# First attention of a two-block transformer kernel: turning the probabilities with a scaled identity, and alternating score and value passes

## The chip, the core and the metric

One core of one Trainium2 chip runs the whole program. The metric is the device time of one execution in microseconds (us). Of the kernel before, three timed runs gave 1631.95, 1635.49 and 1636.21 us; their median is 1635.49 us.

## The reference, cut to what matters

Two transformer blocks run one after the other on 512 tokens of width 1024. The change touches only the attention of the first block: 8 heads of 64 channels, chunks of 64 queries that see their own chunk and the 8 chunks before it, a relative bias, a softmax, and the product with the values.

```python
def one_chunk(c):
    ...
    s = jnp.einsum('bqhd,bkhd->bhqk', qb, kb).astype(jnp.float32) * scale + bias
    valid = (c * CHUNK + kpos - pad) >= 0
    s = jnp.where(valid[None, None], s, NEG_INF)
    p = jax.nn.softmax(s, axis=-1)
    return jnp.einsum('bhqk,bkhd->bqhd', p.astype(vb.dtype), vb)
```

The result goes, beside a pooled half of the channels (`multiscale_pool`), into the output projection `w_out`. Everything is float32.

## The kernel before, in words

**Split matmuls.** A float32 product that must keep its precision is made of three passes (`split3`, lines 347, 350 and 351): both operands are held as a high part and a low part in the type F32R, and the passes are high by high, high by low and low by high, all added up in one PSUM bank. One pass is one weight load (LDWEIGHTS, row PEld of the profile) and one MATMUL. Matmuls on plain F32 operands (`pe.matmul` with `CI(...)`) and transposes (`pe.transpose`) are used where the data isn't split.

**The attention loop.** A unit `u` is one query tile of 128 tokens of one head: `h, q = divmod(u, 4)`, 32 units in all. Its scores are 128 queries by `n = (q + 1) * 128` keys. The loop runs over `u` from 0 to 39 on every engine; each engine has its own list, in order, and semaphores join them. For one `u` TensorE (PE) does:

- `a_scores(u)`: three passes whose contraction has 64 rows (the head's channels; rows 0 to 63 for even heads, 64 to 127 for odd ones), into bank 4 or 5, with `n` columns;
- `side_steps`: one `split3` of 512 columns and 128 rows for the projection `u` (the pooled half), in 24 of the units: not where `u % 10` is 8 or 9, and not from `u = 30` on;
- `a_bias`, once in four units: the next head's bias through a flip matrix, bank 2;
- `a_spread_sums(p)`, at `u` = 11, 19, 27 and 35: the inverse sums of a pair of heads are spread to all partitions by 8 matmuls, bank 2;
- `weigh_values(h, k)` for `u - 7`: three passes with 128 rows and `(4 - k) * 128` columns, into bank 0 or 1;
- `turn_probs` for `u - 2`: `q + 1` transposes of 128x128 of the probabilities `a_p`, bank 6 or 7.

VectorE (DVE) does for one `u`: `a_min_of(u)` (bias added to the scores, minimum of the row; line 1261), then, once in eight units, `a_invert` (reciprocal of 8 columns of sums), `turned_lo(u - 3)` (low part of the turned probabilities, line 1282), and at some units `a_norm` (head output by the inverse sums, line 1276), `a_pair_lo` (line 1288), a part of the pooling, and the weights' low halves (line 1086).

ScalarE (ACT) does `a_expo(u)` (the exponential, line 751, with the sums as a by-product), `turned_hi(u - 2)` (line 759), and at some units `a_spread_copy` (line 770, the spread inverses out of bank 2), `a_pair_hi` (line 774), bias copies and the weights' high halves (line 595).

Behind the loop four `split3` of `poolw` and the eight column tiles of `out1` follow. The second block's attention uses `turn_probs` and `weigh_values` too.

Of the kernel before, what the change touches and what calls it, by code (L numbers as in the profile page):

```python
# [19 lines left out]
ALU = mybir.AluOpType  # L20
# [105 lines left out]
def build(nc, t):  # L126
    with ExitStack() as ctx:
# [68 lines left out]
        with ExitStack() as s:  # L196
# [8 lines left out]
            with ExitStack() as s2:  # L205
                a_s = sb("a_s", [P, 2, S], F32, s2)
                a_p = sb("a_p", [P, 3, S], F32, s2)
                bias = sb("bias", [P, 2, S], F32, s2)
                a_min = sb("a_min", [P, 4 * HEADS], F32, s2)
                a_sum = sb("a_sum", [P, 4 * HEADS], F32, s2)  # L210
                a_rec = sb("a_rec", [P, 4 * HEADS], F32, s2)
                a_full, a_bc = sq, sq_sum
# [246 lines left out]
        a_recip, a_spread, a_spread_out, a_normed = sem("sums_inverted"), sem("inverses_spread"), sem("inverses_copied"), sem("head_out_normed")  # L459
# [88 lines left out]
        def _(act):  # L548
# [217 lines left out]
            def a_spread_copy(p):  # L766
                act.wait_ge(a_spread, p + 1)
                if p >= 2:
                    act.wait_ge(a_normed, 2 * p - 2)
                act.copy(a_bc[:, p % 2, :], bank[2][:]).then_inc(a_spread_out, 1)  # L770

            def a_pair_hi(p):
                act.wait_ge(a_normed, 2 * p + 2)
                act.copy(part[1][:, p, :], a_full[:, p % 2, :]).then_inc(a_ohi, 1)

            for u in range(4 * HEADS + 8):
# [16 lines left out]
            a_pair_hi(3)  # L793
# [274 lines left out]
        def _(dve):  # L1068
# [196 lines left out]
            def a_invert(p):  # L1265

                dve.wait_ge(a_exp, 8 * p + 8)
                dve.reciprocal(a_rec[:, 8 * p:8 * p + 8], a_sum[:, 8 * p:8 * p + 8]).then_inc(a_recip, 1)

            def a_norm(h):  # L1270
                r = 64 * (h % 2)
                dve.wait_ge(a_out, h + 1)
                dve.wait_ge(a_spread_out, h // 2 + 1)
                if h >= 4:
                    dve.wait_ge(a_olo, h // 2 - 1)
                dve.tensor_tensor(a_full[r:r + 64, h // 2 % 2, :], bank[h % 2][r:r + 64, :], a_bc[r:r + 64, h // 2 % 2, :],
                                  ALU.mult).then_inc(a_normed, 1)
# [7 lines left out]

            def a_pair_lo(p):
                dve.wait_ge(a_ohi, p + 1)
                dve.tensor_tensor(part[1][:, 8 + p, :], a_full[:, p % 2, :], part[1][:, p, :].bitcast(F32), ALU.subtract).then_inc(a_olo, 1)
# [14 lines left out]
            for u in range(4 * HEADS + 8):  # L1303
                if u < 4 * HEADS:
                    a_min_of(u)
                if u >= 9 and u % 8 == 1:
                    a_invert(u // 8 - 1)
                if 3 <= u < 4 * HEADS + 3:
                    turned_lo(u - 3, a_thi, a_tlo)
                if u >= 12 and u % 4 == 0 and u % 8 == 4:  # L1310
                    a_norm(2 * (u // 8 - 1))
                if u >= 15 and u % 8 == 7:
                    a_norm(2 * (u // 8 - 1) + 1)
                if u >= 17 and u % 8 == 1:
                    a_pair_lo(u // 8 - 2)
# [6 lines left out]
            a_pair_lo(3)  # L1322
# [463 lines left out]
        def _(pe):  # L1786
# [208 lines left out]
            def a_bias(h):  # L1995
# [4 lines left out]
                if h >= 4 and h % 2 == 0:  # L2000
                    pe.wait_ge(a_spread_out, h // 2 - 1)
# [3 lines left out]
            def a_scores(u):  # L2005
                h, q = divmod(u, TT)
                n, r = (q + 1) * P, 64 * (h % 2)
                if u >= 2:
                    pe.wait_ge(a_biased, u - 1)
                if u == 1:  # L2010
                    pe.wait_ge(acc_free, RES["u"] + 1)
                rows_ = slice(r, r + 64)
                qt, kt = h // 2, 4 + h // 2
                split3(pe, bank[4 + u % 2][:, 0:n], part[1][rows_, qt, q * P:(q + 1) * P], part[1][rows_, 8 + qt, q * P:(q + 1) * P],
                       part[1][rows_, kt, 0:n], part[1][rows_, 8 + kt, 0:n], True, True).then_inc(a_score, 1)

            def a_spread_sums(p):

                pe.wait_ge(a_recip, p + 1)
                pe.wait_ge(b_done, min(2 * p + 4, HEADS))  # L2020
                if p >= 1:
                    pe.wait_ge(a_spread_out, p)
                for q in range(2 * TT):
                    r, c = 64 * (q // TT), q % TT * P
                    mm = pe.matmul(bank[2][r:r + 64, c:c + P], a_rec[:, 8 * p + q:8 * p + q + 1].broadcast_to([P, 64]), CI(C_IDENT),  # L2025
                                   start=True, stop=True)
                mm.then_inc(a_spread, 1)

            def turn_probs(u, probs, ready, lo_sem, done):
# [10 lines left out]
            def weigh_values(h, k, col, lo_sem, done, copied):  # L2040

                if k == 0:
# [3 lines left out]
                mm = split3(pe, bank[h % 2][:, k * P:], part[2][:, k, col:col + P], part[2][:, 4 + k, col:col + P],  # L2046
# [375 lines left out]
```

## Time and profile before

| what | value |
| --- | --- |
| timed runs | 1631.95, 1635.49, 1636.21 us |
| profiled execution, own time | 1633.56 us |
| its span | 1631.8 us |
| TensorE busy over the span | 97% |
| VectorE, ScalarE busy | 48%, 36% |
| first attention, units with score and value passes | about 488.2 to 548 us of the span |
| its last turns and value passes | to 555 us |
| second attention | about 1073 to 1140 us |

The times of the profile are those of one execution. "PE" is the matmul row of TensorE and "PEld" its weight loads. The start of one matmul to the start of the next is the time that the first one took of the engine; the printed duration is longer, because matmuls overlap, and its end is modelled. "128*128 128x512" is 128 rows of contraction by 128 output partitions, then partitions by columns of the moving operand; "64*128" is a contraction over 64 rows.

### The profile page before, as it was taken

Reading aid. Unit: us, or ns where it says so; the run is one execution under the profiler, and the core shown is the slowest. Engines: PE = TensorE matmul, PEld = TensorE weight load, DVE = VectorE, ACT = ScalarE, POOL = GpSimd, SP = SyncE. Lnnn points to the kernel's source line nnn. Section 1 sums busy time; section 2 is a strip of 40 time slices with the busy share of each in tenths; the row PEclk is TensorE's granted clock in tenths of the full one; section 3 lists DMA queues with packets and bytes.
Section 4 is the critical chain, followed back from the end, with each engine's and each line's share of the span. In section 5 each row is a group of like instructions: output and inputs, shape, how many; then the busy total and the mean of one; then the engine's idle time right before and its main releaser. Section 6 shows DMA issues by size and latency. Waiting matters only on the chain.

```text
span 1631.8 us, 19453 instructions
## 1 busy us (share of the span) xinstructions
PE 1580.8 (97%) x7230; PEld 1279.7 (78%) x7230; DVE 789.3 (48%) x1155; ACT 580.8 (36%) x960; POOL 87.7 (5%) x74
## 2 busy tenths in 40 slices
PE   7999999999999999999999989899999999999998
PEld 5888888878867788888888868667777788888886
DVE  6444422455365564444323455687654643234424
ACT  5223212234245533232222263354643434224322
POOL 2000000001012120000000041100000000000000
PEclk9999999999999999999999999999999999999999
DMA  5333343333211133333333333321222232233232
GB/s 161 103 90 103 90 104 90 103 103 110 78 49 40 43 104 101 92 100 93 100 93 100 94 91 91 105 64 42 63 71 101 84 94 97 97 92 101 90 103 91
DMA packets 246028, 147.69 MB, mean 91 GB/s; under 512 B 17472, under 2 KB 230096, under 8 KB 245840
## 3 DMA queue, kind: packets, MB, share of 16 engines
q1 hardware_dynamic: 232896, 141.58, 29.1%
q10 hardware_dynamic: 13072, 5.31, 1.3%
q8 instruction: 38, 0.62, 0.2%
q14 instruction: 22, 0.18, 0.0%
HBM read 142.66 MB, written 4.21 MB: 90 GB/s over the span
## 4 chain that ended last, share of the span: by engine, by line
PE 87%; DVE 8%; ACT 3%; issue 1%; DMA 1%; POOL 0%; DVEq 0%; ACTq 0%; SPq 0%
PE bank L347 28%; PE bank L351 27%; PE bank L350 27%; DVE w_low L1086 3%; ACT w_high L595 1%; DVE region L1097 1%; ACT region L600 1%; PE bank L2037 1%; DMA w_raw<-in_w_out 0%; PE bank L2320 0%; PE bank L1944 0%; ACT sq L608 0%; DVE d_s L1421 0%; DVE c_acc L1444 0%; PE bank L2025 0%
## 5 line engine op out<-in xcount | busy, mean ns | idle before, releaser
L347 PE MATMUL bank<-region,w_high 128*128 128x512 f32 (+1 forms) x1484 | 588.1, 396 | 18.7 <-DVE w_low L1086 11.5
L351 PE MATMUL bank<-region,w_low 128*128 128x512 f32 (+1 forms) x1484 | 579.5, 391 | 0.0
L350 PE MATMUL bank<-region,w_high 128*128 128x512 f32 (+1 forms) x1484 | 579.2, 390 | 0.0
L1086 DVE TENSOR_TENSOR w_low<-w_raw,w_high 128x1024 fp32r<-128x1024 f32 (+1 forms) x259 | 336.1, 1304 | 149.4 <-ACT w_high L595 145.3
L595 ACT CAST w_high<-w_raw 128x1024 fp32r<-128x1024 f32 (+1 forms) x259 | 265.6, 1028 | 261.3 <-DMA w_raw<-in_ffn_w_down 107.4
L347 PEld LDWEIGHTS bank<-region,w_high 128*128 128x128 f32 (+1 forms) x1484 | 278.8, 188 | 91.1 <-DVE w_low L1086 15.5
L351 PEld LDWEIGHTS bank<-region,w_low 128*128 128x128 f32 (+1 forms) x1484 | 278.6, 188 | 60.1
L350 PEld LDWEIGHTS bank<-region,w_high 128*128 128x128 f32 (+1 forms) x1484 | 279.0, 188 | 56.3
L347 PE MATMUL bank<-w_high,region 128*128 128x512 f32 x416 | 168.2, 404 | 8.3 <-DVE rope_y L1387 3.5
L351 PE MATMUL bank<-w_high,region 128*128 128x512 f32 x416 | 165.1, 397 | 0.0
L350 PE MATMUL bank<-w_low,region 128*128 128x512 f32 x416 | 165.0, 397 | 0.0
L643 ACT CAST region<-ff_t 128x512 f32 (+1 forms) x76 | 47.2, 621 | 207.1 <-DVE ff_t L1129 203.4
L1126 DVE TENSOR_TENSOR ff_u<-bank,rstd 128x512 f32<-128x512 f32 x44 | 30.4, 691 | 154.8 <-PE bank L351 154.8
L347 PEld LDWEIGHTS bank<-w_high,region 128*128 128x128 f32 x416 | 79.9, 192 | 28.6 <-DVE w_low L1086 4.1
L351 PEld LDWEIGHTS bank<-w_high,region 128*128 128x128 f32 x416 | 79.8, 192 | 17.3
L350 PEld LDWEIGHTS bank<-w_low,region 128*128 128x128 f32 x416 | 80.0, 192 | 16.0
L1123 DVE TENSOR_TENSOR ff_z<-bank,rstd 128x512 f32<-128x512 f32 x44 | 30.4, 691 | 100.3 <-PE bank L351 92.6
L1156 DVE SCALAR_TENSOR_TENSOR x<-bank,x 128x512 f32<-128x512 f32 x24 | 16.6, 691 | 125.9 <-PE bank L351 125.9
L1137 DVE TENSOR_TENSOR region<-ff_t,region 128x512 f32 (+1 forms) x76 | 52.3, 688 | 50.6 <-ACT region L643 50.6
L633 ACT ACTIVATE ff_s<-ff_z 128x512 f32<-128x512 f32 x44 | 27.9, 634 | 129.5 <-DVE ff_z L1123 129.4
L641 ACT ACTIVATE ff_t<-ff_z 128x512 f32<-128x512 f32 x32 | 20.2, 633 | 105.1 <-DVE ff_z L1135 105.1
L1748 POOL TENSOR_TENSOR sq_sum<-sq_sum,sq 128x512 f32<-128x512 f32 x35 | 47.6, 1361 | 73.6 <-ACT sq L608 73.2
(257 smaller groups left out, 1315.9 us busy)
## 6 DMA issues: line engine op xcount, KB each, us to landing
w_raw<-in_ffn_w_down SPq DMA_DIRECT2D x48, 512.0 KB, 3.9
w_raw<-in_ffn_w_gate SPq DMA_DIRECT2D x44, 512.0 KB, 3.7
w_raw<-in_ffn_w_up SPq DMA_DIRECT2D x44, 512.0 KB, 3.7
w_raw<-in_w_in SPq DMA_DIRECT2D x40, 512.0 KB, 3.8
w_raw<-in_w_up SPq DMA_DIRECT2D x32, 512.0 KB, 4.0
w_raw<-in_w_down SPq DMA_DIRECT2D x32, 512.0 KB, 3.5
w_raw<-in_w_out SPq DMA_DIRECT2D x16, 512.0 KB, 3.8
region_f<-in_x SPq DMA_DIRECT2D x4, 512.0 KB, 5.8
```

The lines of the kernel that those rows point to most:

```text
L347: mm = pe.matmul(out, a_hi, b_hi, start=start, stop=False)
L350: pe.matmul(out, a_hi, b_lo, start=False, stop=False)
L351: return pe.matmul(out, a_lo, b_hi, start=False, stop=stop)
L595: last = act.copy(piece(w_high[b % RING]), piece(w_raw[b % RING]))
L633: act.activation(ff_s[:, j % 2, :], ff_z[:, j % 2, :], ACT.Silu).then_inc(s_ready, 1)
L641: act.activation(ff_t[:, j % 2, :], ff_z[:, j % 2, :], ACT.Square).then_inc(t_ready, 1)
L643: act.copy(dst[:, bass.ds(idx, 1), :] if it is not None else dst[:, idx, :], ff_t[:, j % 2, :]).then_inc(hid_hi, 1)
L1086: last = dve.tensor_tensor(piece(w_low[b % RING]), piece(w_raw[b % RING]), piece(w_high[b % RING]).bitcast(F32), ALU.subtract)
L1123: dve.tensor_tensor(ff_z[:, j % 2, :], bank[r % BANKS][:], rstd[:], ALU.mult).then_inc(z_ready, 1)
L1126: dve.tensor_tensor(ff_u[:, j % 2, :], bank[(r + 1) % BANKS][:], rstd[:], ALU.mult).then_inc(acc_free, 2)
L1137: dve.tensor_tensor(low_of(dst, place, idx, it), ff_t[:, j % 2, :], place.bitcast(F32), ALU.subtract).then_inc(hid_done, 1)
L1748: pool.tensor_tensor(sq_sum[:, which, :], sq_sum[:, which, :], sq[:, i % 2, :], ALU.add).then_inc(sq_added, 1)
```

## The change

Each unit's sums are inverted as soon as its exponential is there, and a 128x128 identity is multiplied by them, row by row (`a_scale`, DVE, once per unit). `turn_probs` no longer transposes: it multiplies the probabilities by that scaled identity in a plain F32 matmul, so that they come out turned and normed. The spread of the sums, its copy, `a_norm` and the pair copies go; ScalarE and VectorE take the high and low part of a head's output straight from its bank (`a_head_hi`, `a_head_lo`). In the loop, the three score passes of unit `u` and the three value passes of unit `u - 7` are issued in turn: score, value, score, value, score, value; the side steps and the bias follow them. The second attention keeps the plain identity and its order, and now gives `turn_probs` its identity in the call; `turn_probs` is a plain matmul there too.

```diff
+            def a_head_hi(h):
+                r = 64 * (h % 2)
+                act.wait_ge(a_out, h + 1)
+                act.copy(part[1][r:r + 64, h // 2, :], bank[h % 2][r:r + 64, :]).then_inc(a_ohi, 1)
...
-                if u >= 11 and u % 8 == 3:
-                    a_spread_copy(u // 8 - 1)
-                if u >= 16 and u % 8 == 0:
-                    a_pair_hi(u // 8 - 2)
+                if u >= 11 and u % TT == 3:
+                    a_head_hi(u // TT - 2)
...
+            def a_scale(u):
+
+                dve.wait_ge(a_exp, u + 1)
+                link(dve.reciprocal(a_rec[:, u:u + 1], a_sum[:, u:u + 1]))
+                if u >= 2:
+                    dve.wait_ge(a_turned, u - 1)
+                dve.tensor_scalar(mix_ident[:, u % 2, :], CI(C_IDENT), a_rec[:, u:u + 1], None, ALU.mult).then_inc(a_scaled, 1)
+
+            def a_head_lo(h):
                 r = 64 * (h % 2)
...
+                dve.wait_ge(a_ohi, h + 1)
+                dve.tensor_tensor(part[1][r:r + 64, 8 + h // 2, :], bank[h % 2][r:r + 64, :], part[1][r:r + 64, h // 2, :].bitcast(F32),
+                                  ALU.subtract).then_inc(a_olo, 1)
...
             for u in range(4 * HEADS + 8):
                 if u < 4 * HEADS:
                     a_min_of(u)
-                if u >= 9 and u % 8 == 1:
-                    a_invert(u // 8 - 1)
+                if 1 <= u <= 4 * HEADS:
+                    a_scale(u - 1)
                 if 3 <= u < 4 * HEADS + 3:
                     turned_lo(u - 3, a_thi, a_tlo)
-                if u >= 12 and u % 4 == 0 and u % 8 == 4:
-                    a_norm(2 * (u // 8 - 1))
-                if u >= 15 and u % 8 == 7:
-                    a_norm(2 * (u // 8 - 1) + 1)
-                if u >= 17 and u % 8 == 1:
-                    a_pair_lo(u // 8 - 2)
+                if u >= 12 and u % TT == 0:
+                    a_head_lo(u // TT - 3)
...
-                    mm = pe.transpose(bank[6 + u % 2][:, place * P:(place + 1) * P], probs[:, k * P:(k + 1) * P], CI(C_IDENT))
+                    mm = pe.matmul(bank[6 + u % 2][:, place * P:(place + 1) * P], probs[:, k * P:(k + 1) * P], ident, start=True, stop=True)
...
             for u in range(4 * HEADS + 8):
+                for pass_ in range(3):
+                    if u < 4 * HEADS:
+                        a_score_pass(u, pass_)
+                    if 7 <= u < 4 * HEADS + 7:
+                        h, k = divmod(u - 7, TT)
+                        weigh_pass(h, k, pass_, P * (h // 2), a_tlo, a_out, a_olo)
                 if u < 4 * HEADS:
-                    a_scores(u)
                     side_steps("u", DT + a_fill(u), DT + a_fill(u + 1), x_in1)
                     if u % TT == 1 and 2 <= u // TT + 1 < HEADS:
                         a_bias(u // TT + 1)
-                if u >= 11 and u % 8 == 3:
-                    a_spread_sums(u // 8 - 1)
-                if 7 <= u < 4 * HEADS + 7:
-                    h, k = divmod(u - 7, TT)
-                    weigh_values(h, k, P * (h // 2), a_tlo, a_out, a_normed)
                 if 2 <= u < 4 * HEADS + 2:
-                    turn_probs(u - 2, a_p[:, (u - 2) % 3, :], a_exp, a_tlo, a_turned)
+                    turn_probs(u - 2, a_p[:, (u - 2) % 3, :], mix_ident[:, u % 2, :], a_scaled, a_tlo, a_turned)
```

`a_score_pass(u, pass_)` and `weigh_pass(h, k, pass_, ...)` hold one pass each of what `a_scores` and `weigh_values` did; the waits stand ahead of pass 0, the signals behind pass 2.

## Rows read from the trace of the kernel before

**Rows 1.** The page: busy time by engine, and the granted TensorE clock in 40 slices
```profile
PE 1580.8 (97%) x7230; PEld 1279.7 (78%) x7230; DVE 789.3 (48%) x1155; ACT 580.8 (36%) x960; POOL 87.7 (5%) x74
PEclk9999999999999999999999999999999999999999
```

**Rows 2.** Windows: stretch, its length, busy us by engine, clock, DMA share, GB/s
```profile
488.20:552.95 64.75, 63.78 (x367) 48.62 (x365) 37.04 (x103) 38.34 (x104) 15.21 (x15) 1.00 0.10 28
552.95:560.14 7.19, 5.45 (x26) 3.85 (x25) 5.08 (x8) 4.87 (x9) 0.00 (x0) 1.00 0.25 73
1198.50:1201.90 3.40, 2.31 (x19) 2.03 (x18) 2.05 (x5) 1.24 (x6) 0.00 (x0) 1.00 0.03 7
1201.90:1205.30 3.40, 3.38 (x8) 2.74 (x9) 1.84 (x7) 2.19 (x6) 0.00 (x0) 0.50 0.43 146
1073.30:1140.20 66.90, 62.07 (x327) 47.35 (x326) 56.56 (x152) 30.29 (x85) 0.00 (x0) 0.97 0.16 48
```

**Rows 3.** Timeline of PE, value projection: start, printed duration, instruction
```profile
467.87 0.39 PE L351 MATMUL bank<-w_high,region 128*128 128x512 f32 x1
468.19 0.50 PE L1977 MATMUL bank<-head_rows,head_select 48*128 48x512 f32 x1
468.61 0.50 PE L347 MATMUL bank<-region,w_high 128*128 128x512 f32 x1
468.95 0.40 PE L350 MATMUL bank<-region,w_high 128*128 128x512 f32 x1
469.18 0.40 PE L351 MATMUL bank<-region,w_low 128*128 128x512 f32 x1
```

**Rows 4.** Timeline in the loop: a unit's scores, 128 columns, then a side step
```profile
501.26 0.32 PE L347 MATMUL bank<-region 64*128 64x128 f32 x1
501.43 0.27 PE L350 MATMUL bank<-region 64*128 64x128 f32 x1
501.54 0.27 PE L351 MATMUL bank<-region 64*128 64x128 f32 x1
501.74 0.50 PE L347 MATMUL bank<-region,w_high 128*128 128x512 f32 x1
502.08 0.39 PE L350 MATMUL bank<-region,w_high 128*128 128x512 f32 x1
```

**Rows 5.** Groups by line: out<-in, shapes, count, busy us, mean ns, idle before
```profile
L2037 PE MATMUL bank<-const,a_p 128*128 128x128 f32 x80 | 14.1, 274 | 0.4 <-DVE region L1282 0.4
L2037 PE MATMUL bank<-const,d_p 128*128 128x128 f32 x40 | 7.3, 281 | 3.9 <-DVE region L1282 3.9
L2025 PE MATMUL bank<-const,a_rec 128*64 128x128 f32 x64 | 6.3, 278 | 0.5 <-issue 0.5
```

**Rows 6.** Chain of waits: start, time that the chain spent there, what
```profile
505.80 0.44 PE bank L2037 x4
518.11 0.52 issue
551.51 1.51 PE bank L2025 x16
1251.54 1.79 PE bank L2320 x16
```

**Rows 7.** Groups by line and shape: DVE and ACT operations of the loop
```profile
L1261 DVE CUSTOM_DVE_ANT_0 a_s<-bank,bias 128x384 f32<-128x384 f32 x8 | 4.4, 556 | 8.8 <-PE bank L351 8.8
L1282 DVE TENSOR_TENSOR region<-bank,region 128x512 fp32r<-128x512 f32 x8 | 5.5, 686 | 0.2 <-ACT region L759 0.2
L759 ACT CAST region<-bank 128x512 fp32r<-128x512 f32 x8 | 4.6, 580 | 4.6 <-PE bank L2037 4.6
L1276 DVE TENSOR_TENSOR sq<-bank,sq_sum 64x512 f32<-64x512 f32 x8 | 5.5, 685 | 1.3 <-PE bank L351 0.7 <-issue 0.5
```

**Rows 8.** Timeline of DVE: an inverse and an identity scaled by it, second block
```profile
1241.64 0.15 DVE L1639 RECIPROCAL mix_r<-mix_std 128x1 f32<-128x1 f32 x1
1241.83 0.29 DVE L1642 TENSOR_SCALAR mix_ident<-const,mix_r 128x128 f32<-128x128 f32 x1
```

More of the change, by code:

```diff
@@ L1321, in _ @@
                     u_tile(u // 10 + 1, bank[3])
-            a_pair_lo(3)
+            a_head_lo(HEADS - 1)
             pooled_lo(3)
@@ L1999, in a_bias, with a_score_pass, turn_probs @@
                     pe.wait_ge(b_done, h)
-                if h >= 4 and h % 2 == 0:
-                    pe.wait_ge(a_spread_out, h // 2 - 1)
                 pe.matmul(bank[2][:, 0:P], toep[:, h % 2, 1, :], CI(C_FLIP), start=True, stop=True)
                 pe.matmul(bank[2][:, P:2 * P], toep[:, h % 2, 0, :], CI(C_FLIP), start=True, stop=True).then_inc(b_mm, 1)
-            def a_scores(u):
+            def a_score_pass(u, pass_):
                 h, q = divmod(u, TT)
                 n, r = (q + 1) * P, 64 * (h % 2)
-                if u >= 2:
+                if pass_ == 0 and u >= 2:
                     pe.wait_ge(a_biased, u - 1)
-                if u == 1:
+                if pass_ == 0 and u == 1:
                     pe.wait_ge(acc_free, RES["u"] + 1)
[L2012 to L2029, printed above, removed]
+                qt, kt = h // 2 + (8 if pass_ == 2 else 0), 4 + h // 2 + (8 if pass_ == 1 else 0)
+                mm = pe.matmul(bank[4 + u % 2][:, 0:n], part[1][r:r + 64, qt, q * P:(q + 1) * P], part[1][r:r + 64, kt, 0:n],
+                               start=pass_ == 0, stop=pass_ == 2)
+                if pass_ == 2:
+                    mm.then_inc(a_score, 1)
+            def turn_probs(u, probs, ident, ready, lo_sem, done):
                 h, q = divmod(u, TT)
@@ L2036, in turn_probs, with weigh_pass @@
                     place = k if h % 2 == 0 else q - k
-                    mm = pe.transpose(bank[6 + u % 2][:, place * P:(place + 1) * P], probs[:, k * P:(k + 1) * P], CI(C_IDENT))
+                    mm = pe.matmul(bank[6 + u % 2][:, place * P:(place + 1) * P], probs[:, k * P:(k + 1) * P], ident, start=True, stop=True)
                 mm.then_inc(done, 1)
-            def weigh_values(h, k, col, lo_sem, done, copied):
-                if k == 0:
+            def weigh_pass(h, k, pass_, col, lo_sem, done, copied):
+                if k == 0 and pass_ == 0:
                     pe.wait_ge(lo_sem, TT * (h + 1))
@@ L2045, in weigh_values @@
                         pe.wait_ge(copied, h - 1)
-                mm = split3(pe, bank[h % 2][:, k * P:], part[2][:, k, col:col + P], part[2][:, 4 + k, col:col + P],
-                            turned_keys(h, k, 0), turned_keys(h, k, 1), k == 0, k == TT - 1)
-                if k == TT - 1:
+                mm = pe.matmul(bank[h % 2][:, k * P:], part[2][:, k + (4 if pass_ == 2 else 0), col:col + P],
+                               turned_keys(h, k, 1 if pass_ == 1 else 0), start=k == 0 and pass_ == 0, stop=k == TT - 1 and pass_ == 2)
+                if k == TT - 1 and pass_ == 2:
                     mm.then_inc(done, 1)
+            def weigh_values(h, k, col, lo_sem, done, copied):
+                for pass_ in range(3):
+                    weigh_pass(h, k, pass_, col, lo_sem, done, copied)
             pe.wait_ge(h_rows_lo, 1)
@@ L2060, in _ @@
             for u in range(4 * HEADS + 8):
+                for pass_ in range(3):
+                    if u < 4 * HEADS:
[3 more added lines that the diff above has]
+                        weigh_pass(h, k, pass_, P * (h // 2), a_tlo, a_out, a_olo)
                 if u < 4 * HEADS:
-                    a_scores(u)
                     side_steps("u", DT + a_fill(u), DT + a_fill(u + 1), x_in1)
@@ L2088, in mixed_in @@
                 else:
-                    pe.wait_ge(a_olo, 4)
+                    pe.wait_ge(a_olo, 2 * k + 2)
             columns("out1", 8, lambda k: parts(1, k if k < 4 else 11 - k), need=mixed_in, order=(7, 6, 5, 4, 0, 1, 2, 3))
@@ L2243, in _ @@
                 if 2 <= w < 4 * DH + 2:
-                    turn_probs(w - 2, d_p[:, 2 * (w - 2) % 6, :], e_prob, e_tlo, e_turned)
+                    turn_probs(w - 2, d_p[:, 2 * (w - 2) % 6, :], CI(C_IDENT), e_prob, e_tlo, e_turned)
                 if w % 2 == 0 or w >= 4 * DH:
```

29 lines of the change are left out of this document (3 added, 26 removed).

## The prediction

> **What bounds the kernel now.** I read the page's busy times first [rows 1]: TensorE (PE) is busy 97% of the span at a granted clock of 9 tenths or more in every slice, VectorE (DVE) 48%, ScalarE (ACT) 36%. Then the windows around the change [rows 2]: in the 64.75 us in which score and value passes meet, PE is busy 63.78 us, DVE 37.04 and ACT 38.34, and the clock is 1.00. So almost every nanosecond that this change gives PE to do or takes from it there moves the end; work on DVE and ACT counts only where PE comes to wait for it. A printed duration of a matmul is no price, since matmuls overlap: I take prices from start to start in the timeline.
>
> **The price of a change of row count.** The timeline of the value projection has one matmul of 48 rows between matmuls of 128 rows [rows 3]. The starts are 467.87, 468.19, 468.61, 468.95, 469.18: steps of 0.32, 0.42, 0.34 and, undisturbed, 0.23 us. Three steps take 1.08 us instead of 0.69, so two changes of row count cost 0.39 us, 0.195 each: some 0.09 behind the matmul before the change and 0.105 on the one after it, whose weight load is no longer hidden. In the attention loop the same is seen for 64 rows [rows 4]: the last score pass has a step of 0.20 where its neighbour has 0.11 (0.09 behind it), and the 512-column side step that follows 0.34 instead of 0.23 (0.11 on it). A first pass of 128 columns has 0.17 against 0.11, only 0.06 on it.
>
> **Part 1, alternating passes.** Before, a unit has score, score, score, and then 128-row work: one change between scores and what follows, one more into the scores from the turning before. After, it is score, value, score, value, score, value: five changes inside where one was, and the side step behind the last value pass needs none. So 4 more per unit. Both kinds of passes are there for u = 7 to 31, 25 units: 100 more changes at 0.195 = 19.5 us. Some of the new changes go into a matmul of 128 columns, which pays about 0.055 less: two for each of the six units of q = 0 (its second and third score pass), three for each of the six of q = 2 (value passes of 128 columns), 30 x 0.055 = 1.7. Left: **+17.8 us**. All lies on PE, which has no slack. The bounds of this term: nothing hides it (19.5), or the engine hides the loads of a regular alternation as it hides those of equal rows, and then it is a gain of some 1.5 us (in 12 units three pairs with 128 columns stand beside 384, where short passes are held at 0.11 by their loads and could run into the longer ones' 0.17 to save some 0.04 a pair). I take 17.8, since the rows of both directions, into and out of fewer rows, agree.
>
> The Trainium skill, in "TensorE: Matmul & The Clock Gate", section "Step-by-step: what each phase is for", says that a weight load is pulled ahead of running matmuls when the row groups don't conflict or when it goes to the background buffer. Read generously (the background buffer serves every load), that rule makes part 1 free; the steps of 0.42 and 0.34 [rows 3] speak against that reading. What it would give is the first rival below.
>
> **Part 2, turning by a matmul.** There are 80 transposes for `a_p` and 40 for `d_p`, one record each [rows 5], and four of them take 0.44 us of the chain [rows 6], 0.11 each. The nearest plain F32 matmul by a scaled identity is the second block's, L2320: 8 matmuls of one token tile stand as x16 and take 1.79 us [rows 6], so it has two passes and costs 0.224. The first attention pays 80 x 0.11 = **+8.8 us**, on PE. In the second attention the call changes too: 40 x 0.11 = 4.4 us, but there DVE is busy 56.56 of 66.90 us and PE 62.07 [rows 2], so PE has 4.8 us of waits in which part of it hides: between 0 and 4.4; I take the middle, **+2.2**, since PE and DVE take turns as the bound.
>
> **Part 3, no spread of the sums.** The spread's 32 matmuls are 64 records [rows 5], 16 for each of four spreads; one takes 1.51 us [rows 6], and the value pass behind it has its load exposed, 0.10 more. Three of them are in the full loop: -3 x 1.61 = -4.8. One wait for the inverses goes too (the 0.52 "issue" ahead of a spread [rows 6], with what surrounds it about 0.7). The fourth spread, at 551.51, covers the last turned unit: ACT needs 0.58 and DVE 0.69 for its two parts [rows 7] before the last head's value passes can start, and only one short value unit (0.35) would cover them then. So of its 1.6 us 0.3 is gained. Together **-5.8 us**. ACT and DVE work that goes with it (copies, `a_norm`, pairs) lies beside PE and gives nothing; only behind the loop one DVE operation of 0.69 [rows 7] leaves the chain of the last head to `poolw`, where PE is busy 5.45 of 7.19 us [rows 2]: **-0.6**.
>
> **Part 4, the new wait: DVE's `a_scale`.** The nearest operations are the same pair in the second block [rows 8]: the inverse of 128x1 starts at 1241.64, the scaled identity at 1241.83 and takes 0.29, 0.48 us in all. The 25 of the full loop are 12.0 us, so that DVE, now busy 37.04 us there [rows 2], would have 49 of some 87 us, 56%, even if nothing went: no bound by its sum. `turn_probs` waits for it a whole unit later: covered. But DVE's order puts it ahead of `turned_lo`, and the alternation moves the first value pass of a head up behind the first score pass. At u = 7, 11, ... 31 this pass waits for `turned_lo(u - 4)`, which DVE does in its step u - 1, behind `a_min_of(u - 1)` and `a_scale(u - 2)`. Counted from the start of unit u - 1 (q = 2, values of 128 columns): the third score pass starts at 0.37 + 0.25 + 0.37 + 0.25 = 1.24 us (each pass with both its changes), DVE starts its minimum some 0.48 later, and needs 0.55, 0.48 and 0.69 [rows 7, 8]: 3.45, with the signal 3.5. PE arrives after the third value pass at 1.77, the side step (0.70), the turning (0.31 with its change) and the first score pass (0.43): 3.2, or 2.5 in units without a side step. Waits of 0.3 in five heads and 1.0 in two (u = 19 and 31): **+3.5 us**. Bounds: 0, if DVE starts earlier than I think, and 8, if 0.5 more comes at each head and the units around the weights' halves stall too. Against it stand about 0.5 us of PE's small waits in the loop [rows 2], which the longer PE work covers: **-0.5**.
>
> **Sum.** 17.8 + 8.8 + 2.2 - 5.8 - 0.6 + 3.5 - 0.5 = 25.4 us. On the profiled execution's own 1633.56 us that is 1659.0; the median of the runs is 1.9 above that execution, inside their own spread of 4.3, so I leave it there: **1659 us**, slower by 1.5%.
>
> **Rivals.**
> - *Loads hidden in the alternation* (the other side). If the engine loads the next weights whatever the rows, when passes alternate and go to different banks, part 1 turns to -1.5 and the waits at the heads shrink, since PE's units don't grow but the third score still comes later: +1. Then 1633.56 + 8.8 + 2.2 - 5.8 - 0.6 - 1.5 + 1.0 - 0.5 = 1637; with the second attention's turning wholly covered 1635, and with plain F32 turning at one pass in effect, 1626. It decides by whether a step of a 512-column score pass is 0.23 or 0.43. For it: in a run of equal rows, 64 or 128, every load is hidden. Against it: each change [rows 3, 4], and no exception that I found in the first attention. 6%.
> - *Half of the exposure.* Only changes into the 64-row passes or out of them stay dear: part 1 is 9 and the time 1650. Against it, both directions show their cost [rows 3]. 8%.
> - *VectorE and its queue as the bound.* The wait for `turned_lo` costs 1 us or more in each head, and the scaled identity is late where DVE also has the weights' low half and the pooled tile: part 4 is 9 to 12, the time 1665 to 1668. For it: several small stages in one queue, in order. Against it: DVE's 56%. 14%.
> - *The clock falls.* After a stretch with PE busy 2.31 of 3.40 us, the granted clock was 0.50 for the next 3.40 us [rows 2], 8 matmuls starting where 14 or 15 would. The alternated units without side steps (8 and 9, 18 and 19, 28 to 31) give PE fewer columns in the same time, though its row of the profile stays full. Each fall costs 1.5 to 2 us; at all three places 5: 1664. 10%. The same page of the Trainium skill ("The HAM clock gate (the "warmup" mystery)") has the clock follow PE's activity between 1.2 and 2.4 GHz; the window just named agrees that it falls to the lower level behind a stretch with less work, and no row shows whether alternated passes do that.
>
> **How the numbers follow.** The forecast holds 62%, the rivals 38. The forecast's own terms leave 1651 to 1666 (part 4 from 0 to 8, the second attention from 0 to 4.4). With the half exposure below and DVE and the clock above, the range for 8 in 10 is 1646 to 1670. A measurement of this kernel tells 0.3%, 5 us, from no change: slower needs over 1640.4. Faster 0.03, same 0.05, slower 0.92; the two small ones are the first rival, and the other cases are all slower.
>
> **What would show it.** Of the profile after: in a unit with 512 columns the six passes start 0.43 us apart, and 0.25 for 128 columns; L2037's successor has 160 records for `a_p` and 80 for `d_p`; no L2025; a weight load that waits for DVE's low part at each head's first value pass, 0.3 to 1 us; the window of the loop grows from 64.75 to about 87 us with PE still over 90% busy at clock 1.00; the second attention longer by 0 to 4.4. The prediction is wrong if passes start 0.23 us apart (the first rival), if waits for DVE come to more than 8 us, or if the clock shows 0.5 in the loop.

## The result, and the profile after

Four runs of the changed kernel gave 1658.59, 1661.40, 1665.40 and 1666.82 us (median 1663.4), four of the kernel before 1633.74 in the median. The ratio is 1.018, with a 95% interval of 1.0165 to 1.0198: slower by 1.8%. The forecast was 1659, slower by 1.5%. The medians differ by 29.7 us. The profiled execution is the fastest of the four, with a span of 1656.8 us against 1631.8: 25.0 more, where the sum of the prediction had 25.4.

The page first, busy times and granted clock, beside [rows 1]:

```profile
PE 1604.9 (97%) x7286; PEld 1295.0 (78%) x7286; DVE 800.4 (48%) x1211; ACT 582.0 (35%) x960; POOL 87.9 (5%) x74
```

PE stays at 97% and has 24 us more to do. Next the windows of the two kernels from the first score pass to the first matmul of `out1`, and from the first to the last turning of the second attention (columns as in [rows 2]). The changed kernel, with two stretches inside its first attention:

```profile
475.85:587.95 112.10, 107.64 (x461) 74.89 (x461) 58.48 (x182) 52.36 (x132) 21.65 (x21) 0.94 0.09 24
530.10:540.40 10.30, 10.06 (x24) 6.49 (x24) 4.64 (x14) 2.92 (x9) 5.05 (x5) 0.50 0.13 31
574.50:577.90 3.40, 3.40 (x10) 2.55 (x10) 1.90 (x8) 1.47 (x4) 0.00 (x0) 0.50 0.00 0
1101.20:1169.70 68.50, 65.29 (x366) 52.18 (x364) 57.03 (x153) 30.26 (x84) 0.00 (x0) 0.98 0.15 47
```

And the same two windows of the kernel before:

```profile
476.35:560.14 83.79, 81.08 (x446) 60.71 (x445) 47.66 (x126) 51.31 (x133) 21.49 (x21) 1.00 0.12 32
1073.20:1139.90 66.70, 61.87 (x326) 47.13 (x324) 56.36 (x152) 30.25 (x84) 0.00 (x0) 0.97 0.16 48
```

The loop itself, from the side step's last pass ahead of the first alternated unit to the first value pass of the last head, as in the first of [rows 2]:

```profile
488.84:581.41 92.57, 89.49 (x372) 61.22 (x370) 46.07 (x150) 39.74 (x105) 15.18 (x15) 0.93 0.08 19
```

So the first attention takes 28.3 us more and the second 1.8 more. The first holds two stretches at half clock (0.50), 10.3 and 3.4 us, which the kernel before doesn't have there. Behind the second attention the changed kernel happens to have less half clock than the profiled execution of before, and gets 4.8 us back; that is why the span grows by 25.0 and not by 30.1. Its other runs have mean clocks of 0.985 to 0.989 where the profiled one has 0.991, and are slower.

The timeline of PE in a unit with 512 columns shows what is paid (start, printed duration, instruction; L1995 is a score pass, L2017 a value pass, L346, L349 and L350 the side step):

```profile
547.18 0.50 PE L1995 MATMUL bank<-region 64*128 64x512 f32 x1
547.68 0.51 PE L2017 MATMUL bank<-region 128*128 128x512 f32 x1
548.12 0.49 PE L1995 MATMUL bank<-region 64*128 64x512 f32 x1
548.54 0.50 PE L2017 MATMUL bank<-region 128*128 128x512 f32 x1
548.97 0.50 PE L1995 MATMUL bank<-region 64*128 64x512 f32 x1
549.39 0.50 PE L2017 MATMUL bank<-region 128*128 128x512 f32 x1
549.73 0.39 PE L346 MATMUL bank<-region,w_high 128*128 128x512 f32 x1
549.96 0.40 PE L349 MATMUL bank<-region,w_high 128*128 128x512 f32 x1
```

From 547.68 the passes start 0.44, 0.42, 0.43 and 0.42 us apart. The last value pass has a change only ahead of it (0.34), and the side step that follows has 0.23, as in [rows 3]. And a unit with 128 score columns and 384 value columns:

```profile
506.08 0.32 PE L1995 MATMUL bank<-region 64*128 64x128 f32 x1
506.34 0.44 PE L2017 MATMUL bank<-region 128*128 128x384 f32 x1
506.71 0.32 PE L1995 MATMUL bank<-region 64*128 64x128 f32 x1
506.96 0.44 PE L2017 MATMUL bank<-region 128*128 128x384 f32 x1
```

The steps are 0.26, 0.37 and 0.25 us, the prices used in part 4. The groups by line have the turning with twice the records of [rows 5], and VectorE's new operation, the scaled identity:

```profile
L2008 PE MATMUL bank<-mix_ident,a_p 128*128 128x128 f32 x160 | 24.6, 288 | 0.0
L2008 PE MATMUL bank<-const,d_p 128*128 128x128 f32 x80 | 12.3, 285 | 3.2 <-DVE region L1273 3.2
...
L1262 DVE TENSOR_SCALAR mix_ident<-const,a_rec 128x128 f32<-128x128 f32 x32 | 11.8, 367 | 1.1
```

Last, PE at unit 19, which has no side step: the first value pass of a head waits for VectorE's low part, and the clock falls at the same moment.

```profile
529.14 0.49 PE L1995 MATMUL bank<-region 64*128 64x512 f32 x1
530.34 0.79 PE L2017 MATMUL bank<-region 128*128 128x512 f32 x1 [0.70 <-DVE region L1273]
531.06 0.79 PE L1995 MATMUL bank<-region 64*128 64x512 f32 x1
531.78 0.79 PE L2017 MATMUL bank<-region 128*128 128x512 f32 x1
```

The step from 529.14 is 1.20 instead of 0.43: a wait of 0.77 us. Behind it, at half clock, the alternated passes start 0.72 apart instead of 0.43, so that a stretch of half clock loses 0.29 / 0.72 = 40% of its length. The 13.7 us here lose 5.5. I use this 40% below to compare alternated kernels as if at one clock: the first attention of the changed kernel is then 106.6 us, 22.8 above before. It is an estimate, and a little low, since a unit is not made of alternated passes alone. A second execution of the same kernel (the first of "The changed kernel again", below) has 13.7 us of half clock between the first value passes of two heads where the profiled one has none: 505.24 to 524.93 there, 502.79 to 516.58 here, 19.69 against 13.79 us, a loss of 43%. By that rate the first attention is 106.2 us, 22.4 above before.

### The profile page after: what moved, and what is told of

It is laid out like the page before. It is cut to its first block, busy times and chain, and to the rows that moved or that the text cites. A ratio compares the mean times of both kernels' runs of the same rounds, so it can differ in the third digit from the quotient of the medians.

```text
span 1656.8 us, 19637 instructions
## 1 busy us (share of the span) xinstructions
PE 1604.9 (97%) x7286; PEld 1295.0 (78%) x7286; DVE 800.4 (48%) x1211; ACT 582.0 (35%) x960; POOL 87.9 (5%) x74
## 4 chain that ended last, share of the span: by engine, by line
PE 86%; DVE 8%; ACT 3%; issue 1%; DMA 1%; POOL 0%; DVEq 0%; ACTq 0%; SPq 0%
PE bank L346 26%; PE bank L350 26%; PE bank L349 26%; DVE w_low L1077 3%; PE bank L2017 2%; PE bank L1995 2%; PE bank L2008 1%; ACT w_high L594 1%; DVE region L1088 1%; ACT region L599 1%; PE bank L2296 0%; PE bank L1927 0%; ACT sq L607 0%; DVE region L1273 0%; DMA w_raw<-in_w_out 0%
## 5 line engine op out<-in xcount | busy, mean ns | idle before, releaser
L346 PE MATMUL bank<-region,w_high 128*128 128x512 f32 (+1 forms) x1484 | 586.3, 395 | 18.0 <-DVE w_low L1077 12.1
L350 PE MATMUL bank<-region,w_low 128*128 128x512 f32 (+1 forms) x1484 | 579.2, 390 | 0.0
L349 PE MATMUL bank<-region,w_high 128*128 128x512 f32 (+1 forms) x1484 | 578.7, 390 | 0.0
L346 PEld LDWEIGHTS bank<-region,w_high 128*128 128x128 f32 (+1 forms) x1484 | 278.7, 188 | 85.6 <-DVE w_low L1077 14.7
L350 PEld LDWEIGHTS bank<-region,w_low 128*128 128x128 f32 (+1 forms) x1484 | 278.5, 188 | 60.3
L349 PEld LDWEIGHTS bank<-region,w_high 128*128 128x128 f32 (+1 forms) x1484 | 278.9, 188 | 56.8
L346 PE MATMUL bank<-w_high,region 128*128 128x512 f32 x416 | 166.1, 399 | 7.0 <-DVE rope_y L1370 3.5
L350 PE MATMUL bank<-w_high,region 128*128 128x512 f32 x416 | 163.2, 392 | 0.0
L349 PE MATMUL bank<-w_low,region 128*128 128x512 f32 x416 | 163.0, 392 | 0.0
L346 PEld LDWEIGHTS bank<-w_high,region 128*128 128x128 f32 x416 | 78.8, 189 | 26.5 <-DVE rope_y L1370 3.9
L350 PEld LDWEIGHTS bank<-w_high,region 128*128 128x128 f32 x416 | 78.6, 189 | 16.9
L349 PEld LDWEIGHTS bank<-w_low,region 128*128 128x128 f32 x416 | 78.9, 190 | 15.5
L1114 DVE TENSOR_TENSOR ff_z<-bank,rstd 128x512 f32<-128x512 f32 x44 | 30.4, 691 | 100.3 <-PE bank L350 92.6
```

Source lines behind the costliest of these rows:

```text
L346: mm = pe.matmul(out, a_hi, b_hi, start=start, stop=False)
L349: pe.matmul(out, a_hi, b_lo, start=False, stop=False)
L350: return pe.matmul(out, a_lo, b_hi, start=False, stop=stop)
L1114: dve.tensor_tensor(ff_z[:, j % 2, :], bank[r % BANKS][:], rstd[:], ALU.mult).then_inc(z_ready, 1)
```

## The experiments

The theory to be tested: a change of row count between neighbouring passes costs PE 0.195 us, whatever else alternates; the second pass of the turning costs 0.11; both are on the bound engine, and the missing spreads and VectorE's queue only trim the sum. The rivals: that alternating banks is the cost, that VectorE is, and, once the trace was seen, that the clock is a cost of its own. "First attention" is the window defined above (before: 83.8 us). Each ratio is to the kernel before, with its 95% interval.

**The old order of passes, with the rest of the change.**

```diff
-                for pass_ in range(3):
-                    if u < 4 * HEADS:
-                        a_score_pass(u, pass_)
-                    ... weigh_pass(h, k, pass_, ...)
+                if u < 4 * HEADS:
+                    for pass_ in range(3):
+                        a_score_pass(u, pass_)
+                    side_steps(...); a_bias(...)
+                ... weigh_values(h, k, ...)
```

> The changed kernel with the old order of passes: three score passes, side step, bias, then three value passes; turning by the scaled identity and everything else of the change stay. Theory (each change of row count costs PE 0.195 us): the 100 extra changes go, and what is left against the kernel before is the second pass of the turning (+8.8 in the first attention, +1.8 in the second) and the missing spreads (-5.8): 3 to 7 us above the kernel before, ratio 1.002 to 1.004, and no half clock inside the first attention. Rival (VectorE's scaling and the order of its queue are what costs, the order of passes is nearly free): 15 us or more above the kernel before, with waits of PE for VectorE.

Measured: ratio 1.0027 (1.0005 to 1.0049), median 1639.1 against 1634.4, 4.7 us. The windows of the two attentions:

```profile
478.33:565.38 87.05, 83.74 (x461) 66.67 (x461) 58.85 (x182) 51.73 (x132) 21.67 (x21) 1.00 0.12 31
1078.68:1147.12 68.44, 65.22 (x364) 52.11 (x363) 56.94 (x153) 30.27 (x84) 0.00 (x0) 0.98 0.16 47
```

The first attention is 3.3 us above before, the second 1.8. VectorE does all of the new work here (58.9 us busy, 58.5 in the changed kernel), and the first attention grows by only 3.3 us: that work is not the price.

**The alternation alone, in the kernel before.**

```diff
-                    a_scores(u)
-                if u >= 11 and u % 8 == 3:
-                    a_spread_sums(u // 8 - 1)
-                    ... weigh_values(h, k, ...)
+                for pass_ in range(3):
+                    ... a_score_pass(u, pass_); weigh_pass(h, k, pass_, ...)
+                side step, bias, spread
```

> The kernel before with the alternated passes alone: transposes, spread of the inverses (moved behind the side step of its unit), norming on VectorE stay. Theory: 100 more changes of row count, +17.8 us with the clock at its upper level, +18 to +25 where the clock falls in the loop as it did in the changed kernel (5.6 us there); ratio 1.011 to 1.015. Six passes of 512 columns start 0.43 us apart. Rival (the turning and VectorE are the cost): within 3 us of the kernel before.

Measured: ratio 1.0132 (1.010 to 1.0163). Its first attention:

```profile
476.82:583.97 107.15, 104.97 (x446) 68.37 (x445) 47.56 (x126) 51.53 (x132) 21.48 (x21) 0.94 0.09 25
```

23.4 us more than before, with 13.7 us of half clock in it, 5.5 lost: 17.9 at equal clock (17.5 at a loss of 43%), where part 1 had 17.8. A wait of 0.5 us at unit 19 is in it: the first value pass of that head starts 0.94 us behind the score pass. The two parts together, 1.0027 and 1.0132, make 1.016 of the changed kernel's 1.018.

**Is it the rows, or the alternating?** Score passes over all 128 rows in the changed kernel, so that each score adds up both heads of a pair and the kernel leaves out keeping them apart:

```diff
-                mm = pe.matmul(bank[4 + u % 2][:, 0:n], part[1][r:r + 64, qt, q * P:(q + 1) * P], part[1][r:r + 64, kt, 0:n],
+                mm = pe.matmul(bank[4 + u % 2][:, 0:n], part[1][:, qt, q * P:(q + 1) * P], part[1][:, kt, 0:n],
```

> The changed kernel with score passes that contract over all 128 rows of the tile instead of the head's 64 (so each score is the sum over both heads of a pair: the part of the computation that this changes). Columns, banks, order and number of matmuls stay; only the row count of a score pass now equals that of a value pass. Theory: 164 changes of row count go, -32 us less 30 to 50 changes into 128 columns at 0.055: -29 us against the changed kernel at equal clock, and the clock has no fall in the first attention (-5.6 more): 4 to 10 us below the kernel before, ratio 0.994 to 0.998; passes of 512 columns start 0.23 us apart. Rival 1 (alternating between two banks or accumulation groups is what exposes the weight loads, rows don't matter): the time of the changed kernel. Rival 2 (VectorE's queue is the next bound): PE comes to wait for VectorE, and the time is between the kernel before and the changed one.

Measured: ratio 1.0003 (0.9985 to 1.0021), median 1635.3. The passes alternate between the same banks as before, and their starts are these:

```profile
537.83 0.39 PE L2017 MATMUL bank<-region 128*128 128x512 f32 x1
538.06 0.40 PE L1995 MATMUL bank<-region 128*128 128x512 f32 x1
538.29 0.39 PE L2017 MATMUL bank<-region 128*128 128x512 f32 x1
538.52 0.39 PE L346 MATMUL bank<-region,w_high 128*128 128x512 f32 x1
```

0.23 us each: the exposed loads are gone, and with them the first rival to this reading. The size was missed: 4 to 10 us below before were expected, and it is level with it. Its window and its waits say why:

```profile
475.68:560.84 85.16, 75.88 (x463) 65.86 (x462) 57.69 (x182) 50.92 (x132) 21.81 (x22) 0.98 0.12 32
```

```profile
PE bank L2017 <- DVE region L1273: 5.1, 8, 1.1
PEld bank L2008 <- DVE mix_ident L1262: 3.5, 3, 2.1
PE bank L2008 <- DVE region L1273: 2.2, 2, 1.9
```

PE is busy 75.9 of 85.2 us. With its work this short, it waits 9.3 us, mostly for VectorE's low parts and scaled identities. VectorE does not bound the changed kernel, but it comes next. The clock is 0.98 in the window and not 1.00 as expected: 3.4 us at half clock stand in it, at about 547 us, behind a wait of the turning of 1.9 us.

**The same in the kernel before.** All its score passes over 128 rows (`rows_` becomes the whole tile), order kept; the two heads of a pair are again added up.

> The kernel before, its order kept, with score passes over all 128 rows instead of the head's 64 (each score is then the sum over both heads of a pair: the part of the computation that this changes). Theory: the 64 changes of row count of the ordered loop go, at 0.195 us less 0.055 for those into 128 columns: 11 to 12 us less in the first attention, if PE stays its bound; VectorE was busy 57% there and would be at 70%, without the scaling that made PE wait 12.5 us in the kernel with alternated passes over 128 rows, so most of it should be kept: ratio 0.993 to 0.996. Rival (VectorE's chain through the minimum, not rows, paced both): less than 5 us are gained.

Measured: ratio 0.9967 (0.9949 to 0.9985), and a first attention of 76.6 us, 7.2 less:

```profile
478.02:554.57 76.55, 70.14 (x447) 59.69 (x446) 47.99 (x126) 50.62 (x132) 21.63 (x22) 1.00 0.13 35
```

PE's busy time falls by 10.9 us (81.1 to 70.1), near the 11 to 12 of the 64 changes; its waits grow from 2.7 to 6.4. The direction and PE's share are as expected, the net gain is smaller by those waits.

**Alternating passes of equal rows.** In the kernel before, value passes take turns with the passes of the side step:

```diff
+    for p_, (a_, b_) in enumerate(((hi, x_hi), (hi, x_lo), (lo, x_hi))):
+        mm = pe.matmul(bank[out][:], a_[:, k, :], b_, ...)
+        if between is not None:
+            between(p_)          # one value pass
```

> The kernel before, with the three value passes alternated with the three passes of the side step instead of following them, in 14 units (not where a spread stands between them). Both have 128 rows, and go to different banks. Theory (the change of row count is what costs): no change, within 1 us over the loop, passes of 512 columns stay at 0.23 us, no half clock in the loop. Rival (alternating between two accumulation groups or banks exposes the loads, whatever the rows): about 5 more exposed loads a unit, 70 in all at 0.2 us, +14 us.

Measured: first attention 83.6 us against 83.8, clock 1.00, PE busy 80.9 against 81.1, in a profiled execution (span 1631.4 us) that is the fastest of ten. The ratio of 1.0022 (0.9997 to 1.0048) can't be told from 1; it alone would still allow several us, and the window decides. Passes of 512 columns in turn (L1992 side, L2051 value):

```profile
510.71 0.40 PE L2051 MATMUL bank<-region 128*128 128x512 f32 x1
510.95 0.40 PE L1992 MATMUL bank<-region,w_high 128*128 128x512 f32 x1
511.19 0.40 PE L2051 MATMUL bank<-region 128*128 128x512 f32 x1
511.42 0.40 PE L1992 MATMUL bank<-region,w_low 128*128 128x512 f32 x1
```

0.24, 0.24 and 0.23 us. Among passes of 128 rows, taking turns between banks and accumulation groups cost nothing here.

**One-pass turning in the second attention of the changed kernel** (`pe.transpose` there, the matmul in the first).

> The changed kernel with the second attention's probabilities turned by one-pass transposes as before. Theory: of the 4.4 us of added passes there about half was hidden in PE's waits for VectorE; the stretch from that attention's first to its last turning, 68.4 us in the changed kernel and 66.6 in the kernel before, goes back to 66.6 (within 0.5, at equal clock). Rival (its passes were hidden, and the 1.8 us come from elsewhere, such as the clock): it stays at 68.4.

Measured in one profiled execution: 66.57 us between the first and the last turning, as before (66.60), against 68.41. So 1.8 to 1.9 of the 4.4 us of added passes are visible there and the rest was hidden in PE's waits, as the middle value of part 2 had it (2.2).

**VectorE's low part ahead of its scaling, in the changed kernel.**

```diff
-                if 1 <= u <= 4 * HEADS:
-                    a_scale(u - 1)
                 if 3 <= u < 4 * HEADS + 3:
                     turned_lo(u - 3, a_thi, a_tlo)
+                if 1 <= u <= 4 * HEADS:
+                    a_scale(u - 1)
```

> The changed kernel with VectorE making the low part of the turned probabilities ahead of the scaled identity in each unit. Theory: the first value pass of a head waits for that low part; in the changed kernel the waits were 0.77 us at units 19 and 31 and 0.49 at unit 11. They shrink by the 0.53 us of inverse and scaling, to 0.25 and 0, and the turning doesn't come to wait, as its identity is wanted a unit later: about 1.3 us less in the first attention at equal clock. Rival (the wait is for the third score pass and VectorE's minimum, not for the scaling): no change, or new waits of the turning for the identity.

Measured, one profiled execution: first attention 106.3 us with 3.4 of half clock, so 104.9 at full clock against 106.6: 1.7 less (1.4 at a loss of 43%; 1.3 were expected). At unit 19:

```profile
529.46 0.49 PE L1995 MATMUL bank<-region 64*128 64x512 f32 x1
530.26 0.50 PE L2017 MATMUL bank<-region 128*128 128x512 f32 x1 [0.31 <-DVE region L1273]
```

A step of 0.80 where 1.20 was: the wait is 0.37, not 0.77. The clock didn't fall at this place in this execution; its one fall, 3.4 us, begins at 570.4, behind the wait of unit 31.

**The changed kernel again,** beside its variants.

> The changed kernel once more, on the chip of its variants. Theory: 1.5 to 2% above the kernel before; if its clock falls inside the first attention come from the order of its passes, they are there in this execution too, at about the same places (units 19 and 31), while the falls behind the second attention may come and go.

Measured: ratio 1.0176 (1.0142 to 1.021), span 1668.3. Its first attention and the half clock in it:

```profile
478.31:597.76 119.45, 115.03 (x462) 80.76 (x461) 58.49 (x182) 52.36 (x132) 21.64 (x21) 0.87 0.09 23
507.40:521.10 13.70, 13.70 (x41) 10.26 (x40) 3.78 (x16) 3.23 (x9) 0.00 (x0) 0.50 0.04 10
538.20:548.40 10.20, 9.71 (x23) 6.34 (x24) 4.90 (x14) 3.18 (x11) 5.05 (x5) 0.50 0.09 24
582.50:589.40 6.90, 6.90 (x26) 5.93 (x26) 3.30 (x10) 2.25 (x5) 0.00 (x0) 0.51 0.01 2
```

30.8 us at half clock, 12.3 lost: 107.1 at full clock, beside 106.6 (106.2 in both at a loss of 43%). Two of the falls are at units 19 and 31, as before; the third, at 507.4, follows the waiting head of unit 11, which has a side step, and wasn't expected. No profiled execution has a fall behind units 8 and 9.

> The changed kernel again, beside its variant with the filling matmuls. Theory: half clock of 10 us or more inside the first attention, its falls behind units 18 and 19 and 28 to 31, first attention 111 to 120 us, whole time 1.5 to 2% above the kernel before.

Measured: ratio 1.0189 (1.0157 to 1.0222), first attention 112.0 us with 13.7 of half clock, behind units 19 and 31.

**Work put into the units without side steps, to hold the clock.**

```diff
+                if fill:      # units 8, 9, 18, 19, 28 to 31
+                    for _ in range(6):
+                        pe.matmul(bank[6 + u % 2][:, 0:2 * P], part[2][:, 0, 0:P], part[2][:, 0, 0:2 * P], start=True, stop=True)
```

> The changed kernel with 6 more matmuls of 256 columns (128 rows, results thrown away, into the bank that the turning overwrites next) in each of the eight units 8, 9, 18, 19, 28 to 31, which have no side step: 0.7 us of PE work each, as much as a side step. Theory of the clock (its falls in the first attention come behind the units without side steps, where exposed loads leave PE few columns in the time): added work of 5.6 us, but no half clock in the first attention, where the changed kernel had 13.7 and 30.7 us of it and lost 5.6 and 12.8 us; the waits of 0.77 us at units 19 and 31 shrink to 0.1. The first attention takes 110 us or less (112.1 and 119.5 in the changed kernel), the whole 1 to 8 us less than the changed kernel. Rival (the falls follow from something else, or from the exposed loads in every unit): the half clock stays and the first attention takes 4 to 5 us more, 116 to 124.

Measured: ratio 1.016 (1.0129 to 1.0192), median 1660.2 beside 1664.4 for the changed kernel. The intervals overlap, so the gain of the whole is not shown; its window has no half clock:

```profile
475.96:586.14 110.18, 107.56 (x509) 76.80 (x509) 57.84 (x182) 52.54 (x132) 21.74 (x21) 1.00 0.10 25
```

Clock 1.00 in the whole first attention, which takes 110.2 us with eight fillings of 0.7 to 0.8 us in it, where the changed kernel takes 112.0, 112.1 and 119.5 without them. That is one profiled execution; the mean clocks of its four runs are 0.991 to 0.994, those of the changed kernel's four 0.984 to 0.991.

This doesn't tell the emptier units from the waits. PE arrives later behind a filling, so the waits at units 19 and 31 shrink from 0.77 us to 0.05 and 0.1, as expected, and every fall in the changed kernel's profiled executions stands at or behind a waiting head (units 11, 19 and 31). Other executions show each of the two alone. A wait without alternated passes: the version with scaled probabilities (next experiment, ordered passes) waits 1.7 us in a turning at 544.4 and has 3.4 us of half clock from about 546; the kernel before and the changed one with the old order of passes have no half clock in their first attention. Alternated passes without a wait: the kernel before with the alternation alone, units 28 and 29, where PE is busy 3.40 of 3.40 us at clock 1.00, in 14 matmuls, and then has 0.52 for 10.2 us:

```profile
559.90:563.30 3.40, 3.40 (x14) 2.12 (x14) 1.97 (x5) 2.59 (x6) 0.00 (x0) 1.00 0.00 0
563.30:573.50 10.20, 10.20 (x24) 5.90 (x25) 4.56 (x12) 3.00 (x9) 4.03 (x4) 0.52 0.00 0
```

How much of the changed kernel's own falls is due to its waits of 0.5 to 0.8 us stays open.

**A version that drops the spreads and keeps one-pass turning.** Ordered passes, `pe.transpose`, and VectorE scales the probabilities themselves:

```diff
-                dve.tensor_scalar(mix_ident[:, u % 2, :], CI(C_IDENT), a_rec[:, u:u + 1], None, ALU.mult).then_inc(a_scaled, 1)
+                n = (u % TT + 1) * P
+                dve.tensor_scalar(a_p[:, u % 3, 0:n], a_p[:, u % 3, 0:n], a_rec[:, u:u + 1], None, ALU.mult).then_inc(a_scaled, 1)
```

> Old order of passes, one-pass transposes in both attentions, no spread of the inverses: VectorE multiplies the probabilities themselves by the inverse sums (128 partitions by 128 to 512 columns, in place) before they are turned. Theory (PE's work is the bound): the spreads' 5.8 us go and nothing is added on PE, some 1.5 us come back as waits (the last head 1.3): 3 to 5 us below the kernel before, ratio 0.997 to 0.998. Rival (the longer chain through VectorE, 0.3 to 0.55 us for a scaling instead of 0.37 for the identity, stalls the turning): as fast as the kernel before or slower.

Measured: ratio 0.9972 (0.995 to 0.9993), median 1632.9 against 1635.4: 0.3% below the kernel before, only just clear of the interval, and well below the changed one. Its first attention takes 81.5 us, 2.3 less, with 3.4 us of half clock in it:

```profile
476.69:558.22 81.53, 76.20 (x382) 56.81 (x381) 61.94 (x182) 51.52 (x132) 22.02 (x21) 0.98 0.13 33
```

PE is busy 4.9 us less, near the 5.8 of the spreads; half of it comes back as waits, most of them for VectorE, busy 61.9 of 81.5 us.

> The kernel with scaled probabilities, ordered passes and transposes, with VectorE's low part ahead of its scaling, as in the variant of the changed kernel that gained 1.6 us. Theory: the turning waited once for 1.8 us where VectorE had the weights' low half and the pooled tile; a low part that is ready earlier frees the bank earlier, 1 to 2 us less in the first attention, ratio to the kernel before 0.996 to 0.998. Rival (scaling is now what comes last): the turning waits for the scaling instead, no gain.

Measured: ratio 0.9979 (0.9959 to 0.9999), first attention 80.4 us at full clock; the version above, less at most half of its 3.4 us of half clock, is 79.8 or more. So no gain: the expected 1 to 2 us didn't come, though the ratio lies in the expected 0.996 to 0.998. The wait of the turning for VectorE's low part is gone (1.7 us before), and in its place the turning waits 2.0 us for the scaled probabilities, as the rival had it.

## Why the prediction was right, point by point

- *What bounds the kernel*: right. PE had 24 us more to do and the span grew by 25.0, while VectorE's 10.8 us more in the first attention cost little by themselves (in the old order everything new together: 3.3 us). The loop takes 92.6 us, 86.7 to 87.1 with the half clock taken out, where about 87 had been said.
- *Part 1, +17.8*: 17.5 to 17.9 measured alone, a wait of 0.5 included. The price per change, from one matmul of 48 rows in another stage [rows 3], held for 64 rows in both directions, and fell only where the rows were made equal.
- *Parts 2 and 3*: the first attention with the old order should have come to 8.8 - 5.8 - 0.6 = +2.4 and came to +3.3; one wait of the turning for VectorE is in it. The second attention took +1.8, not +2.2. The tail is as described: the last head's first value pass starts 1.28 us late, at 581.41.
- *Part 4, +3.5*: the mechanism was right and the size too large. The waits stand in units 19 and 31 (0.77 each, not 1.0) and 11 (0.49), and in the other heads they are 0.07 to 0.18 and not 0.3: 2.4 us in all. At unit 18 the third score pass starts at 528.24 and VectorE its minimum at 528.72, the 0.48 later that was counted; but its operations overlap, the scaling starts at 529.40 and the low part at 529.60, and the value pass can start 2.10 after the score pass where I had added up 2.25. PE is there 0.08 later than I had it. The two make the 0.2 to 0.25 of each head.
- *Sum for the first attention*: 17.8 + 8.8 - 5.8 - 0.6 + 3.5 - 0.5 = 23.2, measured 22.4 to 22.8 at full clock. One bound was added up wrong and decided nothing: with part 4 and the second attention both at 0, the forecast's own terms leave 1653 and not 1651.
- *The clock, the part that was not in the forecast*: the prediction named half clock in the loop as a sign that it is wrong, and that sign came, in every profiled execution of the changed kernel (5.5, 12.3 and 5.5 us lost). By its own words the forecast at clock 1.00 did not hold as a whole; its terms for PE's work and waits did. The measured ratio is 1.018, the forecast's 1.014 to 1.016, by which time of the kernel before is taken. What the clock takes on top was a rival at 10%, with a price of 5 us and a time of 1664, nearer to the measured 1663.4 than 1659 is. Of its three places two were right, and units 8 and 9 were not. The page called "TensorE: Matmul & The Clock Gate" of the Trainium skill, in its section on the HAM clock gate, has the clock follow activity. The filled variant fits that: more work and shorter waits, no fall.
- *Luck*: the half clock of the profiled execution was masked by less of it behind the second attention (4.8 us), which is why 25.0 agreed so well with 25.4. The medians, 29.7 us apart, don't have that luck; that the rest of their distance is the clock too is argued from the lower mean clocks of the slower runs and not shown.

## What to carry to other kernels

In this kernel each change between passes of 64 or 48 rows and passes of 128 rows cost PE about 0.2 us, half of it behind the old pass and half on the new one (less where the new one has 128 columns). Sort passes by row count before interleaving them; among passes of 128 rows interleaving was free. A plain F32 matmul by an identity has two passes where a transpose has one, so folding a scale into the identity must buy back more than 0.11 us a block. Scaling the probabilities on VectorE added no pass to PE, but half of what the dropped spreads saved came back as waits. Read start-to-start steps, and the clock of each stage, before trusting the sum of a whole span.

## What the runs showed of the hardware that I had not expected

The same scaled identity took VectorE 285 ns at its shortest and 808 at its longest. All seven above 0.30 us overlap an operation of GpSimd's pooling; so does one that took 0.29 us (at 480.17), so the overlap alone doesn't decide it. DVE and then GpSimd in the changed kernel, timeline:

```profile
498.09 0.81 DVE L1262 TENSOR_SCALAR mix_ident<-const,a_rec 128x128 f32<-128x128 f32 x1
501.42 0.71 DVE L1262 TENSOR_SCALAR mix_ident<-const,a_rec 128x128 f32<-128x128 f32 x1
```

```profile
497.78 1.04 POOL L1749 TENSOR_TENSOR win<-u_pad 128x512 f32<-128x512 f32 x1 [15.05 <-issue]
498.89 2.16 POOL L1749 TENSOR_TENSOR win<-win 128x512 f32<-128x512 f32 x2
501.44 1.49 POOL L1752 TENSOR_SCALAR win<-win 128x512 f32<-128x512 f32 x1
```

The mean of the 32 is 367 ns, so this added 32 x 0.08 = 2.6 us to VectorE. The "GPSIMD Engine Reference" of the Trainium skill, section "Specifications", says that the two engines share their SBUF interfaces and contend for some VectorE instructions. The rows agree that there is contention; they don't show whether it is those interfaces. The wait of unit 11 (0.49 us) has such a long scaling right ahead of it, at 501.42.
